# A hybrid encoder layer on one core: projections and values of the recurrences turned by VectorE blocks through DRAM, a doubled scratch, and input chunks split later

## What is computed

```
h = x + 0.5 * SwiGLU1(rms(x))
P = rms(h) @ W_in                       # columns: RWKV | DeltaNet | two gates
A = rwkv7(P[rwkv])                      # 16 heads x 64, token shift, delta-rule state, chunks of 64
B = gated_deltanet(P[gdn])              # 8 value heads x 128, conv4 on q, k, v, chunks of 64
h = h + W_out(sigmoid(GA)*(A @ LA) + sigmoid(GB)*(B @ LB))
h = h + cross_attention(rms(h), rms(mem))
h = h + 0.5 * SwiGLU2(rms(h));  y = rms_final(h)
```

## Time and profile before

| | us |
|---|---|
| median of 3 runs | 2677.63 (2676.46 to 2682.86) |
| the profiled execution, its own time | 2678.46 |
| its span, first to last instruction | 2676.7 |
| TensorE busy in the span | 2641.7 (99%) |
| VectorE busy | 1549.9 (58%) |
| ScalarE busy | 1218.4 (46%) |

### The profile page before, as it was taken

One profiled execution on the slowest core, in us unless ns is written; L12 is line 12 of the kernel. 1 busy time (PEld: TensorE's weight loads), 2 busy tenths in 40 slices (PEclk: granted clock), 3 DMA queues, 4 the chain that ended last, 5 costly groups with the idle time before them and its releaser, 6 DMA issues.

```text
span 2676.7 us, 36323 instructions
## 1 busy us (share of the span) xinstructions
PE 2641.7 (99%) x14357; PEld 2175.9 (81%) x14357; DVE 1549.9 (58%) x1788; ACT 1218.4 (46%) x1395; POOL 162.4 (6%) x300
## 2 busy tenths in 40 slices
PE   8999999999999999999999999999999999999998
PEld 7888888888888777888887887788888888888886
DVE  5555555555567776748556766555655555555444
ACT  5444444444456447355455544333444444444343
POOL 2000000000000000000001112000100000000000
PEclk9999999999999999999999999999999999999999
DMA  6767677767676554454578878654766767677664
GB/s 225 224 212 221 218 216 219 215 207 211 190 215 192 173 182 151 148 163 133 171 268 237 247 236 249 207 156 141 226 208 213 224 211 222 210 226 222 196 191 148
DMA packets 275178, 543.50 MB, mean 203 GB/s; under 512 B 21660, under 2 KB 32064, under 8 KB 274672
## 3 DMA queue, kind: packets, MB, share of 16 engines
q1 hardware_dynamic: 250256, 469.69, 56.8%
q0 software_dynamic: 19872, 62.66, 8.0%
q10 hardware_dynamic: 4928, 9.45, 1.0%
HBM read 506.05 MB, written 35.67 MB: 202 GB/s over the span
## 4 chain that ended last, share of the span: by engine, by line
PE 46%; DMA 5%; DVE 2%; issue 1%; ACT 1%; POOL 1%; SPq 0%; DVEq 0%; POOLq 0%; ACTq 0%
PE pp L327 14%; PE pp L329 14%; PE pp L328 14%; DMA hid_dram<-hid_t 1%; DMA xq<-hid_dram 1%; DMA raw<-in_w_lift 1%; DVE wlo L288 1%; DMA kt_m<-hid_dram 1%; PE pa L1951 1%; PE pb L1936 1%; POOL xq L546 0%; ACT whi L283 0%; DMA gs<-proj 0%; POOL kt_m L546 0%; PE pa L380 0%
## 5 line engine op out<-in xcount | busy, mean ns | idle before, releaser
L288 DVE TENSOR_TENSOR wlo<-raw,whi 128x1024 fp32r<-128x1024 f32 (+1 forms) x888 | 1077.8, 1219 | 943.4 <-ACT whi L283 936.1
L283 ACT ACTIVATE whi<-raw 128x1024 fp32r<-128x1024 f32 (+1 forms) x888 | 934.9, 1057 | 1297.6 <-PE pp L329 1215.6
L327 PE MATMUL pp<-whi,xhi 128*128 128x512 f32 (+1 forms) x2208 | 869.4, 394 | 0.7 <-DVE xlo L411 0.7
L328 PE MATMUL pp<-whi,xlo 128*128 128x512 f32 (+1 forms) x2208 | 857.5, 388 | 0.0
L329 PE MATMUL pp<-wlo,xhi 128*128 128x512 f32 (+1 forms) x2208 | 857.4, 388 | 0.0
L327 PEld LDWEIGHTS pp<-whi,xhi 128*128 128x128 f32 x2208 | 414.7, 188 | 92.9 <-issue 7.2
L329 PEld LDWEIGHTS pp<-wlo,xhi 128*128 128x128 f32 x2208 | 414.7, 188 | 86.0
L328 PEld LDWEIGHTS pp<-whi,xlo 128*128 128x128 f32 x2208 | 414.9, 188 | 82.1
L327 PE MATMUL pp<-whi,hhi 128*128 128x512 f32 x704 | 273.9, 389 | 0.0
L328 PE MATMUL pp<-whi,hlo 128*128 128x512 f32 x704 | 273.9, 389 | 0.0
L329 PE MATMUL pp<-wlo,hhi 128*128 128x512 f32 x704 | 273.9, 389 | 0.0
(11 more groups left out here) (431 smaller groups left out, 2036.5 us busy)
## 6 DMA issues: line engine op xcount, KB each, us to landing
raw<-in_ffn_w_gate SPq DMA_DIRECT2D x176, 512.0 KB, 4.3
raw<-in_ffn_w_up SPq DMA_DIRECT2D x176, 512.0 KB, 4.5
raw<-in_ffn_w_down SPq DMA_DIRECT2D x176, 512.0 KB, 4.1
raw<-in_w_in SPq DMA_DIRECT2D x144, 512.0 KB, 3.8
hid_dram<-hid_t POOLq DMA_DIRECT2D x43, 512.0 KB, 3.3
xq<-hid_dram POOLq DMA_DIRECT2D x156, 128.0 KB, 4.8
raw<-in_w_lift SPq DMA_DIRECT2D x32, 512.0 KB, 6.3
raw<-in_w_out SPq DMA_DIRECT2D x32, 512.0 KB, 5.1
```

The source lines that it names most:

```text
L283: nc.scalar.activation(whi[:, s, :, 0:width], raw[:, s, :, 0:width], ACT.Copy).then_inc(whi_ready, 1)
L288: nc.vector.tensor_tensor(wlo[:, s, :, 0:width], raw[:, s, :, 0:width], whi[:, s, :, 0:width].bitcast(F32), ALU.subtract).then_inc(wlo_rea ...
L327: nc.tensor.matmul(out, a_hi[:, k0 + k, tok], w_hi, start=first, stop=False)
L328: nc.tensor.matmul(out, a_lo[:, k0 + k, tok], w_hi, start=False, stop=False)
```

## The change

Six things, in the order of the diff:

1. The tables `STEPS`, `SLOTS_ACT`, `SLOTS_DVE` are new: 252 steps instead of 236 lie at named points, 20 instead of 36 at `rest`.
2. `hid_dram` is two scratches, used in turn, and the store has a semaphore of its own (`hid_stored`): `turn_out` may store a tile while the fetches of the one before are in flight. Only its own fetches wait for them.
3. Eight of the 17 spooled products (`TURNED`, all that a recurrence reads except the gate z) are written into the spool block by block (L373), turned in place by VectorE in 32x32 blocks (`spool_turn`, L383), stored by ScalarE three slots later than before (`spool_store`, L390) and fetched with four transfers of 32 partitions each. `moved_take` copies them from `gs`, `nat` or `vnat` with two copies. The eight `mix_turn` of these projections are gone from TensorE.
4. The values of all four halves are turned by VectorE (two operations of 512 elements per partition, L1382 and L1738), stored in `v_dram` with four transfers and fetched with one (`values`). The transposes at L1148 and the third block of L1488 are gone, with VectorE's copy `vn_r`; `vb` is now made from the fetched tile.
5. In `lift`, `plain_hi` and `plain_lo` of chunk c-2 stand behind the products of chunk c instead of ahead of its merge; in the product after it they stand two slots later.
6. In `mkv`, `x_moved_hi` and `x_moved_lo` of a query chunk stand two slots later.

The core of the diff:

```diff
-        hid_dram = nc.dram_tensor("hid_dram", (P, 1024), F32, kind="Internal").ap()
+        hid_dram = nc.dram_tensor("hid_dram", (2, P, 1024), F32, kind="Internal").ap()
...
+        TURNED = (0, 1, 3, 4, 5, 6, 7, 8)
...
                 split_hi(act, BG[q]["slot"], j)
                 if j == 4 and q > 0:
-                    spool_out(act, q - 1, spool)
+                    spool_out(act, q - 1)
+                if j == 7 and q > 0 and q - 1 in TURNED:
+                    spool_store(act, q - 1)
...
+            if q in TURNED:
+                by_block = spool_blocks(q).rearrange("p (b k t j) -> p k b t j", b=4, k=4, t=TT)
+                for tt in range(TT):
+                    op = nc.scalar.activation(by_block[:, :, :, tt, :], pp[:, 2 * pr["par"] + tt, :].rearrange("p (k b j) -> p k b j", k=4, b=4),
+                                              ACT.Copy, scale=rstd[:, tt:tt + 1])
...
+        def spool_turn(dve, q):
+            dve.wait_ge(sem(BG[q]["released"][0]), BG[q]["released"][1])
+            nc.vector.transpose(spool_blocks(q), spool_blocks(q)).then_inc(sem("spool_turned"), 1)
...
+        def spool_store(act, q):
+            act.wait_ge(sem("spool_turned"), TURNED.index(q) + 1)
+            act.dma_start(turned_proj(q), spool_blocks(q)).then_inc(sem("spooled"), 16)
...
+                split_lo(dve, BG[q]["slot"], j)
+                if j == 6 and q > 0 and q - 1 in TURNED:
+                    spool_turn(dve, q - 1)
...
+            scratch = hid_dram[d % 2]
             pool.wait_ge(sem("hid_turned"), d + 1)
+            nc.gpsimd.dma_start(scratch, hid_t[:, :, :, :].rearrange("p b m j -> p (b m j)")).then_inc(sem("hid_stored"), 16)
+            pool.wait_ge(sem("hid_stored"), 16 * d + 16)
             if d > 0:
-                pool.wait_ge(sem("hid_moved"), 80 * d)
-            nc.gpsimd.dma_start(hid_dram[:, :], hid_t[:, :, :, :].rearrange("p b m j -> p (b m j)")).then_inc(sem("hid_moved"), 16)
-            pool.wait_ge(sem("hid_moved"), 80 * d + 16)
+                pool.wait_ge(sem("hid_moved"), 64 * d)
...
+        def moved_take(act, dst, src, ready, m):
+
+            act.wait_ge(*ready)
+            blocks = src[:, :, :].rearrange("p t c -> p (t c)").rearrange("p (q k t j) -> p k t q j", q=4, k=4, t=TT)
+            for tt in range(TT):
+                op = copy(act, dst[:, :, tt * P:(tt + 1) * P].rearrange("p k (q j) -> p k q j", q=4), blocks[:, :, tt, :, :])
...
-                mix_turn(pe, 2, gs, (sem("gs_loaded"), 16))
                 bg_pe(pe, "gdn1.v")
-                mix_turn(pe, 3, vnat, (sem("vnat_loaded"), 16))
...
-            mix_turn(pe, m0, gs, (sem("gs_loaded"), 16 * (2 + 2 * hf)))
-            bg_pe(pe, f"rw{hf}.r")
-            mix_turn(pe, m0 + 1, nat, (sem("nat_loaded"), 16 * n))
-            bg_pe(pe, f"rw{hf}.k")
-            mix_turn(pe, m0 + 2, gs, (sem("gs_loaded"), 16 * (3 + 2 * hf)))
...
+            dve.wait_ge(sem("v_moved"), 80 * hf + 64)
             link(dve, v_.scalar_tensor_tensor(full[:, :, :], units[2], -1.0, dec[:, :, :], ALU.mult, ALU.mult))
...
+            def values(n, parts, dst, *free):
+
+                pool.wait_ge(sem("v_turned"), n + 1)
+                if n > 0:
+                    pool.wait_ge(sem("v_moved"), 80 * n)
+                for b, (rows, src) in enumerate(parts):
+                    g.dma_start(v_dram[32 * b:32 * b + 32, :].rearrange("i (k e) -> k i e", k=rows), src).then_inc(sem("v_moved"), 16)
+                pool.wait_ge(sem("v_moved"), 80 * n + 64)
+                for name, value in free:
+                    pool.wait_ge(sem(name), value)
+                g.dma_start(dst, v_dram[:, :]).then_inc(sem("v_moved"), 16)
...
-                    if 2 <= c < NDC + 2 and j == 6:
-                        x_moved_hi(act, "qnorm", c - 2, "mem_q_norm")
+                    if 3 <= c < NDC + 3 and j == 0:
+                        x_moved_hi(act, "qnorm", c - 3, "mem_q_norm")
```

Of the tables, two lines of the first RWKV half show the manner (`r`, `k` and `v` are the points between the three `mix_turn`; their steps are now in `g`):

```diff
-    "rw0.lora": 4, "rw0.g": 1, "rw0.r": 1, "rw0.k": 3, "rw0.v": 5, "rw0.kk": 5, "rw0.tilde": 9, "rw0.nat": 1,
+    "rw0.lora": 4, "rw0.g": 13, "rw0.kk": 5, "rw0.tilde": 11, "rw0.nat": 2, "rw0.mats0": 3, "rw0.mats1": 3,
```

More of the change, by code:

```diff
@@ L967, in invert_pe, with invert_act @@
                 bg_pe(pe, f"inv{v}.4{lane}")
-        def invert_act(act, v, lanes, spool):
-            bg_act(act, f"inv{v}.rows", spool)
+        def invert_act(act, v, lanes):
+            bg_act(act, f"inv{v}.rows")
             for lane, use, (x, y, m, r_, f) in lanes:
@@ L1144, in gdn_pe @@
                 for p, r in enumerate(halves):
-                    nc.tensor.matmul(heads4[2][r, c, :], qk[:, 2 + p, tok], ident[:, :], start=True, stop=True)
-                for e in range(2):
-                    for p, r in enumerate(halves):
-                        mm = nc.tensor.matmul(heads4[c // 2][r, 2 * (c % 2) + e, :], vg[:, 2 * p + e, tok], ident[:, :], start=True, stop=True)
+                    mm = nc.tensor.matmul(heads4[2][r, c, :], qk[:, 2 + p, tok], ident[:, :], start=True, stop=True)
             mm.then_inc(sem("g_naturals"), 1)
@@ L1339, in gdn_dve @@
             v_.tensor_scalar(dec[:, :, :], dec[:, :, :], 0.0, None, ALU.min).then_inc(sem("g_diff"), 1)
+            bg("values")
+            dve.wait_ge(sem("g_vact"), n)
+            dve.wait_ge(sem("g_conv"), 2 * n)
+            for th in range(2):
+                op = v_.transpose(vt_g[:, th, :, :, :, :].rearrange("p a e c j -> p (a e) c j"),
+                                  vg[:, :, :].rearrange("p h (c x i) -> p h c x i", x=2, i=32)[:, :, :, th, :])
+            op.then_inc(sem("v_turned"), 1)
             bg("norms")
@@ L1354, in gdn_dve @@
             v_.tensor_tensor(dec[:, :, :], dec[:, :, :], over_units(m_inc), ALU.mult).then_inc(sem("g_dec"), 1)
-            bg("vb")
-            for b in range(2):
-                own = be_n[:, hf, 4 * b:4 * b + 4].unsqueeze(2).to_broadcast([P, 4, GH])
-                v_.tensor_tensor(vb[:, 2 * b:2 * b + 2, :].rearrange("p c (e d) -> p (c e) d", d=GH), heads4[b], own, ALU.mult)
             bg("naturals")
@@ L1372, in queries @@
             def queries():
+                dve.wait_ge(sem("v_moved"), 80 * n)
+                for e in range(2):
+                    own = be_n[:, hf, :].rearrange("p (c e) -> p c e", e=2)[:, :, e:e + 1].unsqueeze(3).to_broadcast([P, NCH, 4, 32])
+                    v_.tensor_tensor(vb[:, :, e * GH:(e + 1) * GH].rearrange("p c (q j) -> p c q j", q=4),
+                                     v_tok[:, :, e, :, :].rearrange("p q c j -> p c q j"), own, ALU.mult)
                 dve.wait_ge(sem("g_exps"), 2 * n)
@@ L1479, in rw_pe @@
             pe.wait_ge(sem("r_tilde"), n)
-            for src, out, need in ((bt, spread[1], None), (kt, spread[0], ("r_bonus_out", n)), (tmp[2], spread[1], ("r_nat", 3 * hf + 1))):
+            for src, out, need in ((bt, spread[1], None), (kt, spread[0], ("r_bonus_out", n))):
                 if need is not None:
@@ L1687, in rw_dve @@
             op.then_inc(sem("r_cum"), 1)
+            bg("values")
+            for th in range(2):
+                op = v_.transpose(vt_r[:, th, :, :, :], v__[:, :, :].rearrange("p d (c x i) -> p d c x i", x=2, i=32)[:, :, :, th, :])
+            op.then_inc(sem("v_turned"), 1)
             bg("kk")
@@ L2248, in fetch @@
                     pool.wait_ge(sem(name), value)
-                g.dma_start(dst[:, :, :], proj[q].rearrange("(t p) c -> p t c", p=P)).then_inc(sem(loaded), 16)
+                if q in TURNED:
+                    blocks = dst[:, :, :].rearrange("p t c -> p (t c)").rearrange("p (q e) -> p q e", q=4)
+                    for b in range(4):
+                        g.dma_start(blocks[32 * b:32 * b + 32, :, :],
+                                    turned_proj(q).rearrange("(q i) e -> i q e", q=4)[:, :, 256 * b:256 * b + 256]).then_inc(sem(loaded), 16)
+                else:
+                    g.dma_start(dst[:, :, :], proj[q].rearrange("(t p) c -> p t c", p=P)).then_inc(sem(loaded), 16)
             def fetch_z(src):
@@ L2254, in fetch_z, with delta_values, rwkv_values @@
                     g.dma_start(zg[r, :, :], src.rearrange("(c t) d -> t c d", t=C)[:, :, p * 2 * GH:(p + 1) * 2 * GH]).then_inc(sem("z_loaded"), 16)
+            def values(n, parts, dst, *free):
[8 more added lines that the diff above has]
+                g.dma_start(dst, v_dram[:, :]).then_inc(sem("v_moved"), 16)
+            def delta_values(hf):
+                parts = [(4, vt_g[:, th, p, :, :, :].rearrange("p e c j -> p (e c j)")) for p in range(2) for th in range(2)]
+                values(hf, parts, v_tok[:, :, :, :, :].rearrange("p q e c j -> p (q e c j)"),
+                       ("mix_turned", 2) if hf == 0 else ("g_out_turned", 1))
+            def rwkv_values(hf):
+                parts = [(2, vt_r[r, th, :, :, :].rearrange("p d c j -> p (d c j)")) for r in halves for th in range(2)]
```

(2 more changed lines are left out.)

156 lines of the change are left out of this document (88 added, 68 removed), and 56 rows, old and new, of tables (SLOTS_DVE, STEPS).

## The result

| | before | changed |
|---|---|---|
| median (lowest to highest) | 2677.93 (2676.46 to 2682.86) | 2657.76 (2654.72 to 2660.11) |
| executions | 4 | 4 |
| the profiled execution | 2678.46 | 2654.72 |
| its span | 2676.7 | 2653.0 |

The ratio of the times is 0.9924, with a 95% interval from 0.9907 to 0.9940: 20.2 us faster between the medians, 23.7 between the two profiled spans. The forecast was 2652.

What follows compares the result with a forecast made beforehand. TensorE, busy 99% of the span, was taken as the bound. 15 - 1 (recurrences) + 2.0 + 1.7 (lift) + 8.1 (mkv) = 25.8 us off 2678.5 gave 2652.7, stated as 2652; likeliest 2645 to 2658, full range 2643 to 2667.

Steps and rivals of the forecast that it cites:

- the likeliest case: The forecast itself for the whole kernel: 2652 us, range 2645 to 2658, chance 0.64.
- Work taken off TensorE, 15 us: Recurrences: projection turns 7.1, DeltaNet values 3.5, RWKV values 4.0 us removed, 14.6 together, taken as 15.
- I take 5 after, 1 more: Recurrences, 800 to 1350 us: TensorE's waits go from 4.0 to 5 us, bounds 0 and 16.
- rival A: Recurrences bound by VectorE, so TensorE's 15 us return as waits and the time is 2666; chance 0.18.
- 12 us, against some 15 us ... work between: Values' DRAM trip: 2.2 issue, 4.8 landing, 0.7 and 4.3 fetch, 12 us, against some 15 us of VectorE and TensorE work.
- rival B: Recurrences: DRAM trips are waited for, over 4 us at each of eight; time 2686 at that price; chance 0.08.
- GpSimd's added work blocks nobody: Recurrences: GpSimd is busy 20 of 550 us, so some 24 us more there block nobody.
- The tight place, v in the RWKV halves: RWKV halves: v's fetch after r's take, 8.3 us, fits ScalarE's 8.7 us between takes; hidden with 0.9 us to spare.
- `lift`, 2.0 of 4.0 and half of the clock: lift: 2.0 of 4.0 us of stalls gone (bounds 0 and 4), plus 1.7 us of slow clock (bounds 0 and 3.4).
- `mkv`, 8.1: mkv: all stalls, 6.7 us, and the 1.7 us clock loss go, rounded down to 8.1; bounds 4 and 8.4.
- The one or the other nearly alone: mkv: ScalarE's 7.16 us wait for xq needs only the second scratch or the two-slot-later splits, nearly alone.
- C: lift and mkv: stalls stay because they are DMA, not order; time 2664.5; chance 0.10, for all or part of it.

Runs made afterwards that it cites:

- a2: Changed kernel with the DeltaNet values turned by TensorE again, RWKV values still by the trip: ratio 0.9891 to the kernel before, median 2651.17, recurrences 526.6 us.
- p1: Kernel before with each of the eight mix_turn of spooled projections done twice on TensorE, back to back: ratio 1.0004, recurrences 540.8 us.
- p2: Kernel before with each of the eight mix_turn done twice and one background step between the two: ratio 1.0033, recurrences 548.3 us.
- c0: The changed kernel run once more, nothing altered: ratio 0.9926 to the kernel before, median 2660.57, recurrences 531.7 us.
- a1: Changed kernel with VectorE's wait for the landed store of the DeltaNet values moved behind the mask operations: ratio 0.9922 to the kernel before, recurrences 531.7 us.
- a2b: Repeat of a2 (changed kernel, DeltaNet values turned by TensorE) as base of the next two runs: ratio 0.9904 to the kernel before, recurrences 526.5 us.
- a4: a2b with GpSimd fetching the second DeltaNet half's two row tiles behind its second projection instead of ahead: ratio 0.9892 to the kernel before, median 2651.68.
- s2: Kernel before with only the query chunks' splits two slots later in mkv: ratio 0.9977, nhi stretch 179.4 us instead of 183.6.
- a3: a2b with the RWKV values turned by TensorE too, so no value takes the DRAM trip: ratio 0.9926 to the kernel before, recurrences 533.2 us.
- s3: Kernel before with only lift's splits moved behind the merge and its weight splits: ratio 0.9984, lift 87.1 us instead of 94.5.
- s1: Kernel before with only the two scratches and the store's own semaphore: ratio 0.9958, nhi stretch 173.4 us instead of 183.6.
- s4: Kernel before with the two scratches and the later splits in lift and mkv, recurrences untouched: ratio 0.9942, median 2664.43.

## Why the prediction was right, and where its steps weren't

**The direction and the size** came out: 2657.8 against 2652, inside the likeliest case's range (2645 to 2658) by a hair, faster by 20.2 us where 25.8 were summed. That it came so near is partly luck: the recurrences gave 8.5 us less than summed, `lift` and `mkv` 5.9 more.

**Work taken off TensorE, 15 us.** Right. a2 undoes only the DeltaNet values' part of the work; what is left removed is 7.1 + 4.0 = 11.1, and the recurrences are 9.7 shorter than before, with 0.9 us more of idle time. The turn's price was measured apart (0.87 to 0.91 by starts, in p1 and p2).

**"I take 5 after, 1 more."** This is the step that failed. The idle time rose by 6.8 us (4.0 to 10.8), and the slow clock behind the longest stall took 1.4 more (3.70 for a block of 2.26): 8.2 instead of 1, within the bounds that I gave. c0 comes to 9.0 by idle time alone, without the slow clock. The sign that I named, idle time under 8 us in 800 to 1350, was missed (10.8), without reaching the 15 of rival A. I priced VectorE's added work and looked for the loss there, on its chains. It came from the trips instead.

**"12 us, against some 15 us ... work between."** The values' trip was mis-sized and one of its waits left out. It took 19.5 us: the four stores begin 2.0 us behind the turn, are issued over 2.81 us from 953.57 and land 8.1 us after the last (964.5); the fetch lands 6 us behind its issue, with the four fetches of `gs` right behind it in the queue. I had taken 4.8 and 4.3 from transfers of other shapes. And I counted only the end of the trip; the wait for its store ahead of the mask, which stands in the diff, was not on my list. a1 shows that this omission alone changes little: take this wait away and the later one takes its place. a2 and a2b show the whole: with no trip the recurrences are 4 to 5 us shorter, although TensorE has 3.5 us of work more, and the medians fall by more than that. That is rival B in its mechanism, at two of the places, and too small to decide.

**The fetches beside the weights.** I wrote that GpSimd's added work blocks nobody. Its instructions don't; its transfers do. `gs`, `gr`, `bb` and the weights meet in 870 to 885 us, and TensorE waits 2.16 us for a copy behind a late split. a4 takes the row tiles out of the crowd and the wait goes. That the fetch of `gs` falls there because the spool is stored later is only argued, from its wait of 13.59 us for `proj<-spool_g`.

**The tight place, v in the RWKV halves.** Hidden, as worked out: in 800 to 1350 us ScalarE has no wait for `gs` among its waits, and TensorE's own there are below 0.6 us each. In the kernel before, TensorE waited 0.8 us for this fetch, and up to 2.3 in s2; that is gone. The values' trip of the RWKV halves is hidden as well, and a3 shows that it is worth its price.

**`lift`, 2.0 of 4.0 and half of the clock.** Too low. All of it went (a wait of 1 to 2 us was expected to stay), and s3 shows that the order alone does it. The bound of 4 + 3.4 was the value of that profile. In the times it is worth 4.3, since the profile of before was an extreme one.

**`mkv`, 8.1.** Mis-sized by 2: 10.2 by the starts. The signs came true: clock 1.00, no wait for `wlo`, and GpSimd's stores no longer wait for `xq<-hid_dram`. TensorE's idle time undercounts a stall. A bar of 0.39 us ends after the next start would come (0.225), so each of the four stalls loses some 0.17 more than its idle time, 0.7 in all. The count says 289 against 243, 46 x 0.225 = 10.4 us. Of the difference to 8.4 some 1.3 stays open. "The one or the other nearly alone" was half right: the scratch alone is enough (s1), the later split alone gets 4.2 of the 10.2 (s2).

**The rivals.** A (VectorE bounds the recurrences) fell as a whole: VectorE's busy time in them rose by 12.3 us without a wait for `wlo`, and behind the largest added waits stand transfers. A small part of it, the added turns in the chain of the DeltaNet halves, is not excluded. C (the stalls stay) fell to s1 and s3. A page's rule bears on B: the Trainium skill ("VectorE: DVE Perf Modes", section Rules for kernel authors) leaves a transpose of 128x128 to TensorE when its result may lie in PSUM. The projections are such turns, and there the runs don't agree with it: their trips gain 3.4 us (a3 against s4). The values are smaller blocks, of which the rule doesn't speak: of 128x64 in the DeltaNet halves, where TensorE is the better choice (a2, a2b against c0), and of 64x64 in the RWKV halves, where it isn't (a3 is 6.7 us slower than a2b in the recurrences). What differs between the two is the time at hand: in the first RWKV half the values are turned at 1070.4 us, fetched from 1096.2 on, and first read by TensorE at 1146.0.

## What to carry to other kernels

Work moved off the bounding engine is worth its start-to-start time only where its replacement is back in time: price a trip through DRAM by a transfer of the same shape, from the turn to the landed fetch, list every wait that its memory brings, and ask for each use apart, since one half of the same edit can pay and the other cost. Let one stage's edits be judged by the starts of its first and last matmul (or by their count), not by idle time, and over several executions, because a stall where the transfers are busy (DMA share 0.8 to 0.9 here) moves from stage to stage. Price an operation by the starts around it and not by how much longer its stage becomes: more work can also hide a wait. A wait for the fetches before one's own store is taken away by a second scratch, and that was the best part of this change.

## What the hardware showed that was not expected

- The stall of `lift` is not at a fixed place: with the old order the stage took 94.5, 88.2, 89.2, 89.0 and 89.1 us in five kernels, and the product behind it 88.0, 92.0, 92.2, 89.8 and 92.0.
- Eight transposes directly behind eight others cost 0.87 to 0.91 us, about what a block on its own costs between matmuls (0.89 to 1.05); but eight such blocks made the recurrences only 4.5 us longer, since waits went.
- Four stores of the values (128 KB each) landed 8.1 us after the last was issued (6.4 us from issue to landing is the median of all eight), where the fetches of `xq`, of the same size, took 4.8.
- A wait of 2.54 us ahead of L946 was followed by a lower clock (3.70 us for what takes 2.26). The same block in c0, behind a wait of 2.31, kept full clock (2.26 us), and so did L983 behind one of 2.16.
